# Three experts with at most 64 tokens in two passes, and one VectorE operation for the low part of each 1 MB load

## What is computed

```python
def swiglu(h, w1, w3, w2):
    return (jax.nn.silu(h @ w1) * (h @ w3)) @ w2

def moe_ffn(h, router, w1, w3, w2):
    t = h.reshape(B * S, D)                        # 256 x 1024
    logits = (t @ router).astype(jnp.float32)
    top_v, top_i = lax.top_k(logits, TOP_K)        # 2 of 8
    top_w = jax.nn.softmax(top_v, axis=-1)
    gates = jnp.sum(jax.nn.one_hot(top_i, N_EXPERTS) * top_w[..., None], axis=1)
    out = jnp.zeros_like(t)
    for e in range(N_EXPERTS):                     # D_FF_EXPERT = 3584
        out = out + gates[:, e:e + 1] * swiglu(t, w1[e], w3[e], w2[e])
    return out
```

## Time and profile before

| | us |
|---|---|
| median of 3 runs (1663.34 to 1664.61) | 1664.23 |
| the profiled execution's own time | 1664.06 |
| its span | 1662.0 |
| TensorE busy (matmuls) | 1616.8 |
| VectorE busy | 1300.9 |
| ScalarE busy | 1098.5 |
| GpSimd busy | 30.0 |

### The profile page before, as it was taken

The page is one execution under the profiler, slowest core; times in us unless marked ns, Lnnn a source line. Parts: engine busy times, 40 slices in busy tenths (PEclk is TensorE's granted clock), DMA queues, the critical chain, the costliest instruction groups (busy, mean ns, idle before and its releaser), DMA issues.

```text
span 1662.0 us, 23002 instructions
## 1 busy us (share of the span) xinstructions
PE 1616.8 (97%) x9056; PEld 1387.2 (83%) x9056; DVE 1300.9 (78%) x1411; ACT 1098.5 (66%) x1257; POOL 30.0 (2%) x37
## 2 busy tenths in 40 slices
PE   5999999999999996999999999999999999999998
PEld 5999869999899965888788788788788788788786
DVE  4887744555688654989889889889889889889886
ACT  4775343333567614878778778778778778778785
POOL 3000000000000003000000000000000000000000
PEclk9999999999999998999999999999999999999999
DMA  9555365555455547999999999999999999999990
GB/s 236 177 167 181 109 202 178 190 191 179 133 173 176 174 160 289 350 345 374 350 336 373 352 335 368 351 340 366 364 332 375 352 334 371 355 336 370 355 361 26
DMA packets 231398, 460.55 MB, mean 277 GB/s; under 512 B 7434, under 2 KB 79478, under 8 KB 231286
## 3 DMA queue, kind: packets, MB, share of 16 engines
q1 hardware_dynamic: 230262, 457.21, 78.1%
q0 software_dynamic: 832, 1.74, 0.7%
q10 hardware_dynamic: 192, 0.08, 0.0%
HBM read 457.96 MB, written 1.05 MB: 276 GB/s over the span
## 4 chain that ended last, share of the span: by engine, by line
PE 88%; DVE 4%; ACT 4%; DMA 3%; issue 1%; SPq 0%; ACTq 0%; DVEq 0%
PE bank L935 18%; PE bank L936 18%; PE bank L939 18%; PE bank L700 8%; PE bank L701 8%; PE bank L702 8%; PE bank L745 2%; PE bank L963 2%; DMA ring<-in_w_in 2%; PE bank L970 2%; PE bank L997 1%; ACT w_hi L507 1%; DVE w_lo L515 1%; DMA arena<-in_moe_w 1%; DVE shared8k L1685 1%; DVE prod L1683 1%
## 5 line engine op out<-in xcount | busy, mean ns | idle before, releaser
L551 DVE TENSOR_TENSOR w_lo<-arena,w_hi 128x1024 fp32r<-128x1024 f32 x486 | 579.4, 1220 | 82.3 <-ACT w_hi L545 70.8
L545 ACT ACTIVATE w_hi<-arena 128x1024 fp32r<-128x1024 f32 x492 | 517.7, 1061 | 168.7 <-PE bank L939 148.4
L935 PE MATMUL bank<-w_hi,h_hi 128*128 128x512 f32 x896 | 359.2, 401 | 3.2 <-DVE h_lo L1769 3.2
L936 PE MATMUL bank<-w_hi,h_lo 128*128 128x512 f32 x896 | 349.8, 390 | 0.0
L515 DVE TENSOR_TENSOR w_lo<-ring,w_hi 128x2048 fp32r<-128x2048 f32 x89 | 203.7, 2290 | 161.5 <-ACT w_hi L507 160.4
L700 PE MATMUL bank<-h_hi,w_hi 128*128 128x256 f32 x992 | 284.4, 287 | 8.0 <-DVE w_lo L515 6.3
L701 PE MATMUL bank<-h_lo,w_hi 128*128 128x256 f32 x992 | 281.6, 284 | 0.0
L702 PE MATMUL bank<-h_hi,w_lo 128*128 128x256 f32 x992 | 281.5, 284 | 0.0
L939 PE MATMUL bank<-w_lo,h_hi 128*128 128x512 f32 x896 | 276.9, 390 | 0.0
L507 ACT ACTIVATE w_hi<-ring 128x2048 fp32r<-128x2048 f32 x89 | 170.3, 1913 | 131.0 <-PE bank L702 80.8
L551 DVE TENSOR_TENSOR w_lo<-ring,w_hi 128x1024 fp32r<-128x1024 f32 x180 | 215.1, 1221 | 26.7 <-ACT w_hi L545 22.9
(11 more groups left out here) (239 smaller groups left out, 1659.8 us busy)
## 6 DMA issues: line engine op xcount, KB each, us to landing
arena<-in_moe_w SPq DMA_DIRECT2D x246, 1024.0 KB, 6.1
ring<-in_moe_w SPq DMA_DIRECT2D x90, 1024.0 KB, 6.4
ring<-in_ffn_w SPq DMA_DIRECT2D x33, 1024.0 KB, 5.2
ring<-in_w_gate SPq DMA_DIRECT2D x32, 1024.0 KB, 5.3
ring<-in_w_in SPq DMA_DIRECT2D x16, 1024.0 KB, 5.6
ring<-in_w_branch SPq DMA_DIRECT2D x8, 1024.0 KB, 4.8
ring<-in_w_out SPq DMA_DIRECT2D x8, 1024.0 KB, 4.8
x_tok<-in_x SPq DMA_DIRECT2D x2, 512.0 KB, 4.2
```

The lines of the kernel that those rows point to most:

```text
L545: nc.scalar.activation(half_hi[:, m % AHEAD, :], raw_of(n)[:, HALF * (m % 2):HALF * (m % 2) + HALF], ACT.Copy)\
L551: eng.tensor_tensor(half_lo[:, m % AHEAD, :], raw_of(m // 2)[:, HALF * (m % 2):HALF * (m % 2) + HALF], half_hi[:, m % AHEAD, :].bitcast(F3 ...
L935: pe.matmul(dst, hi, w[:, cols], start=first(x), stop=False)
L936: pe.matmul(dst, lo, w[:, cols], start=False, stop=False)
```

## The change

Expert 0 stays first. The other seven are put in an order that the counts set: the three with the fewest tokens go to positions 2, 4 and 6 (`SMALL`), the rest to 1, 3, 5 and 7. VectorE works out the order (the kernel's `order`, `perm` and `onehot`), permutes the columns of `chosen`, `place` and `gate` (`arrange`), and SyncE reads the expert's number from SBUF and puts it in the load's address (`expert`, `expert_drams`). `most_i` becomes the larger of the highest count and twice the third smallest of the seven, so that the same `If` with 128 also asks whether three of them have at most 64 tokens.

In positions 2, 4 and 6 the tokens take 64 columns. The gather writes them twice, the high part goes to columns 0 to 63 of `h_hi` and the low part to columns 64 to 127 of the same tile. One matmul with `w_hi` then gives hi by hi in rows 0 to 63 and lo by hi in rows 64 to 127; one with `w_lo` adds the rest. A half is four matmuls (`half_few`) where it was six. The two row groups have to be added. For h3 and w2 of such an expert that is done by later matmuls (`fold` in place of `ident`, and the spread with the gates written twice). For h1 it has to be done ahead of silu: ScalarE copies rows 64 to 127 to `prod`, VectorE adds rows 0 to 63, and ScalarE makes silu twice, for the upper and the lower rows.

VectorE's low part is made for a load at once (`split_load_lo`, 2048 columns), after both its halves have a high part; GpSimd's three first loads likewise. At the kernel's start unit 2 of `w_in` is issued ahead of the constants and parameters, and GpSimd's small loads wait for unit 1.

```diff
-        def split_half_lo(eng, m):
-            eng.wait_ge(half_hi_done, m + 1)
-            eng.tensor_tensor(half_lo[:, m % AHEAD, :], raw_of(m // 2)[:, HALF * (m % 2):HALF * (m % 2) + HALF],
-                              half_hi[:, m % AHEAD, :].bitcast(F32), ALU.subtract)\
-                .then_inc(half_lo_pool if ex.by_pool(m) else half_lo_dve, 1)
+        def split_load_lo(eng, n):
+            eng.wait_ge(half_hi_done, 2 * n + 2)
+            eng.tensor_tensor(w_lo[:, n % LO, :], raw_of(n), w_hi[:, n % HI, :].bitcast(F32), ALU.subtract)\
+                .then_inc(half_lo_pool if ex.by_pool(n) else half_lo_dve, 1)
...
-                if n == 2:
-                    sp.dma_start(par_rows[PC_CW:PC, :, :], conv_w.rearrange("l t (h p) -> (t h) l p", p=P)).then_inc(rows_loaded, 16)
...
                 sp.dma_start(ring[:, n % SLOTS, :].rearrange("p (k c) -> p k c", k=src.shape[1]), src)\
                     .then_inc(loaded[n % SLOTS], 16)
+                if n == 2:
+                    sp.dma_start(const[:, P:C_N], table[:, P:C_N]).then_inc(const_loaded, 16)
+                    sp.dma_start(par_rows[PC_CW:PC, :, :], conv_w.rearrange("l t (h p) -> (t h) l p", p=P)).then_inc(rows_loaded, 16)
...
+            def expert(e):
+                if e not in values:
+                    sp.wait_ge(perm_ready, 1)
+                    values[e] = sp.value_load(perm_i[0:1, e:e + 1], min_val=1, max_val=E - 1)
+                return values[e]
...
-                    for m in (2 * (n - RAW), 2 * (n - RAW) + 1):
-                        wait_half_lo(sp, m)
+                    wait_half_lo(sp, 2 * (n - RAW))
...
-            pool.wait_ge(loaded[0], 16)
+            pool.wait_ge(loaded[1], 16)
...
+            def half_few(m, outs, first, final):
+                pe.wait_ge(half_hi_done, m + 1)
+                w, wl = half_hi[:, m % AHEAD, :], half_lo[:, m % AHEAD, :]
+                for x, (both, cols, dst) in enumerate(outs):
+                    pe.matmul(dst, both, w[:, cols], start=first(x), stop=False)
+                wait_half_lo(pe, m)
+                for x, (both, cols, dst) in enumerate(outs):
+                    last = pe.matmul(dst, both, wl[:, cols], start=False, stop=final(x))
+                last.then_inc(half_used, 1)
...
# ScalarE
                     if done == ("h1", 1, 1):
                         act_e.wait_ge(half_used, u + 1)
+                        if i // S_MOE in SMALL:
+                            fn(prod[0:FEW, i % 2, :], bank[4 + i % 2][FEW:P, :], ACT.Copy).then_inc(z_copied, 1)
...
+                    if done == ("h3", 0, 1) and i // S_MOE in SMALL:
+                        act_e.wait_ge(z_added, few_steps(i) + 1)
...
+                        fn(sil[0:FEW, i % 2, :], prod[0:FEW, i % 2, :], ACT.Silu)
+                        fn(sil[FEW:P, i % 2, :], prod[0:FEW, i % 2, :], ACT.Silu).then_inc(sil_done, 1)
...
# VectorE
+            step(stt(out=cnt, in0=iota[:, 1:E], scalar=1.0 / 16, in1=counts[:, 1:E], op0=ALU.mult, op1=ALU.add))
...
+            ts(most_i[:, :], third[:, :], CAP / FEW, most[:, 0:1], ALU.mult, ALU.max).then_inc(most_ready, 1)
...
+                    if done == ("h3", 0, 0) and i // S_MOE in SMALL:
+                        dve.wait_ge(z_copied, few_steps(i) + 1)
+                        tt(prod[0:FEW, i % 2, :], bank[4 + i % 2][0:FEW, :], prod[0:FEW, i % 2, :], ALU.add).then_inc(z_added, 1)
                     if done == ("h3", 0, 0) and i >= 1:
                         lower(i - 1)
```

More of the change, by code:

```diff
@@ L46 @@
 AHEAD = 6
+SMALL = (2, 4, 6)
+FEW = 64
 MORE = 8
@@ L84, in shape_constants @@
     c[:, C_IOTA:C_IOTA + P] = np.arange(P)
+    by_count = list(SMALL) + [p for p in range(1, E) if p not in SMALL]
+    for r, p in enumerate(by_count):
+        c[:, C_WANT + p - 1] = r
     return c
@@ L359, in trunk_kernel @@
         most_i = sb("most_i", [P, 1], I32)
+        perm_i = sb("perm_i", [P, E], I32)
+        chosen_p = sb("chosen_p", [P, TT, E + 2])
+        place_p = sb("place_p", [P, TT, E + 2])
+        gate_p = sb("gate_p", [P, TT, E + 2])
+        third = sb("third", [P, 1])
+        OTHERS = E - 1
+        scratch = [prod[:, 1, 128 * i:128 * i + 128] for i in range(4)]
+        cnt = scratch[0][:, 0:OTHERS]
+        order = scratch[0][:, 16:16 + OTHERS]
+        last_small = scratch[0][:, 32:32 + OTHERS]
+        perm = scratch[0][:, 48:48 + OTHERS]
+        more = scratch[1][:, 0:OTHERS * OTHERS].rearrange("p (a b) -> p a b", a=OTHERS)
+        onehot = scratch[2][:, 0:OTHERS * OTHERS].rearrange("p (a b) -> p a b", a=OTHERS)
+        moved = scratch[3][:, 0:TT * OTHERS * OTHERS].rearrange("p (t a b) -> p t a b", t=TT, a=OTHERS)
         lgT = qk_raw[0:E, 0, :, :].rearrange("p i c -> p (i c)")[:, 0:T]
@@ L535, in wait_half_lo, with few_steps @@
         def wait_half_lo(eng, m):
-            eng.wait_ge(half_lo_pool if ex.by_pool(m) else half_lo_dve, ex.lo_count(m))
+            eng.wait_ge(half_lo_pool if ex.by_pool(m // 2) else half_lo_dve, ex.lo_count(m // 2))
+        def few_steps(i):
+            return sum(x // S_MOE in SMALL for x in range(i))
         def split_half_hi(m):
@@ L668, in _ @@
                                    pattern=[[0, 4], [-1, P]], channel_multiplier=1).then_inc(ws_lower, 1)
-            for m in range(ex.halves):
-                if ex.by_pool(m):
-                    split_half_lo(pool, m)
+            for n in range(len(ex.loads)):
+                if ex.by_pool(n):
+                    split_load_lo(pool, n)
         @block.tensor
```

173 lines of the change are left out of this document (133 added, 40 removed).

## The result

| | before | changed |
|---|---|---|
| median, us | 1663.78 (4 runs, 1663.06 to 1664.61) | 1647.88 (4 runs, 1645.52 to 1651.56) |
| profiled execution's span, us | 1662.0 | 1645.4 |
| mean granted clock of TensorE in that span | 0.992 | 0.984 |

The ratio is 0.9906, 95% interval 0.9887 to 0.9926: 15.9 us faster. The forecast was 1638.3 us, in a range of 1612 to 1658. The sign and the loop that holds the small steps came out as written, the gain is 16 us and not 26. The four runs of the changed kernel spread over 6 us. The four of before lie within 1.6, but 19 more of before, taken beside the first experiments, spread over 6 us too (1660.14 to 1666.29), so the spread is no mark of the change.

A forecast was written before the change was run, and what follows sets the result against it. TensorE bounds the kernel before; in small steps a VectorE and ScalarE loop of 16.65 us would. Small experts -24.8, start -2, normalization +1 make -25.8 against 1664.06: 1638.3 us, range 1612 to 1658.

The forecast's parts named there:

- The pace of the small steps: Small experts' steps: a VectorE and ScalarE loop of 16.65 us sets the pace, above TensorE's 12.4 and DMA's 16.3.
- the three signs of being wrong: ScalarE waits for loads in small experts, the clock is under 1.00 there, or normal experts take over 126 us.
- first matmul to the end of the first addition: Small expert's first step: from TensorE's first matmul to VectorE's first addition of the row groups, 8.9 us.
- six bare loops: Small expert: six loops of 16.65 us, each six low parts 13.2, product 0.60, addition 0.65, silu and high part 2.2.
- after the last addition, to the next expert: Small expert's end: 2.2 us, a low part of 2.2 and its matmuls of 1.35, 5.75 us in all.
- silu "0.50 us each by 923.03 - 922.53": Small steps: ScalarE makes silu twice after VectorE's addition, each taken as 0.50 us, within the 2.2 us before the low part.
- Rival 3: Small steps: TensorE's clock falls and the kernel is slower, 1685 us at two thirds of matmuls slow, 1753 at all; 7%.
- the point from which it decides: Share of a small step's matmuls at the lower clock where TensorE passes 16.65 us (0.44) or 17.85 us (0.56).
- the -2: Kernel's start: 2 us gained from the new load order, bounds 8.7 gained and 3 lost.
- The +1 for the normalization: Ahead of the experts: normalization waits for GpSimd's operations of twice the length, between 0 and 2.4 us, 1 lost taken.
- Rival 1: Small steps: tighter loop at VectorE's bare sum of 14.8 us, 1604 us, or likelier half of it, 1621; 16%.
- Rival 2: Looser loop, 0.9 us more wait per small step (1657 us), or the 0.8 us cover in normal steps fails (1649); 14%.

The follow-up runs named there:

- the filled kernel: Changed kernel plus TensorE matmuls whose results nobody reads, in every step of the small experts: 1643.68 us, ratio 0.9873; again 1643.78 us, 0.9882.
- The start alone: Kernel of before with only the new order of the loads at the start: 1660.47 us, ratio 0.9975.
- the merge alone: Kernel of before with only low parts of 2048 columns, on VectorE and GpSimd: 1664.06 us, ratio 1.000.

## Why the prediction was right, and where it was off

**The pace of the small steps: right.** They are VectorE's and ScalarE's loop, not TensorE's (12.4 us) and not DMA's. The wait stands where it was put, behind two silus and a high part: 2.09 us where some 1.8 were named. TensorE waits for VectorE there, and ScalarE for VectorE's addition and for no load. Of the three signs of being wrong that the prediction names, one came: the clock is 0.95 in the six loops and not 1.00. The other two did not (no wait for loads, 124.89 us for a normal expert). ScalarE's waits in the first small expert (892 to 1025; total, times, longest):

```profile
ACT qk_raw L1390 <- DVE prod L1940: 16.2, 7, 2.9
ACT w_hi L577 <- PE bank L975: 4.5, 10, 0.8
```

The addition is 0.60 from start to start (993.98 - 993.37), 0.65 was taken.

**A small expert: 122.17 us, not 118.0** (the first of the three, from its first matmul at 895.88 to the next expert's at 1018.05). Term by term:

| term | predicted | measured |
|---|---|---|
| first matmul to the end of the first addition | 8.9 | 9.2 |
| extra operations in six loops | 3.4 | 3.4 |
| six bare loops | 99.9 (16.65 each) | 101.5 (16.92 each) |
| TensorE's clock in the first loop | 0 | 0.9 |
| after the last addition, to the next expert | 5.75 | 6.33, and 0.8 with the clock low |
| sum | 118.0 | 122.1 |

(6.33 is from the filled kernel, where the same stretch runs at full clock: 1013.64 - 1007.31. The 0.8 is this expert's alone: behind the other two the clock did not fall.) The next expert should have spared 1.3 us, 1.8 for the matmuls less 0.5 for a late low part. From its first matmul to its gathering it takes 64.40 us in the filled kernel (1013.64 to 1078.04), a normal one 65.22 (770.99 to 836.21): 0.82 less. The late low part is there; what was left out is that eight transposes with `fold` take 0.81 us where four took 0.36.

The mis-sized term of the loop is **silu "0.50 us each by 923.03 - 922.53"**. That row is a silu on 128 rows. The new ones, on 64 rows and the same 512 columns, stand 0.65 us apart (994.08, 994.73, 995.38). Two of them make 0.30 us a loop more, which covers 16.92 - 16.65 = 0.27, and it is on the way out once more. The records themselves are nearly as long, 0.63 us against 0.60; the 128-row operation's successor starts 0.10 us before its end, the 64-row silu's 0.02 after. The old silu read PSUM and the new ones read SBUF, but a 64-row copy from PSUM has the same 0.62 from start to start (900.07, 900.69). Why was not tried.

**Rival 3 had its mechanism right and its place wrong.** The step that failed is the sentence that "the rows of this case show no swing at waits under 2 us". Between the first expert's first matmul at 657.79 and 1648 us the trace of before has no wait of TensorE at all, so its silence was no evidence. In the changed kernel the clock fell after waits of 1.77 to 2.05 us. The rule cited there, from the Trainium skill ("TensorE: Matmul & The Clock Gate", section "A second HAM failure mode: psum-queue depth-cycling"), that frequent short idle stretches make the clock swing, is borne out by the trace. But the price was 3.8 us and not 21 to 90: the falls were short, and in the middle steps they lay in TensorE's slack. The prediction had the point from which it decides (44% of a step's matmuls at the lower level); the middle steps stayed under it, and it did not ask about the first and the last step, where a fall costs at once (0.9 us in the first loop, 0.8 on the one way out where it came).

**The sum.** The experts gained 12.6 us in the trace where 24.8 was forecast. Of the 12.2 that are missing, silu's size took 18 x 0.27 = 4.9, the clock 3.8, the way in and out of three experts 3 x 0.88 = 2.6, and the next expert's first step 3 x 0.48 = 1.4. That is 0.5 too much, and the five normal experts give most of it back, 124.89 us each in place of 124.96. Ahead of the experts -1 was forecast (-2 and +1), and the two traces give -4.0, so an error the other way made up for some 3 us of this. The start alone measured -3.4 us, so the -2 was too small, inside its bounds of -8.7 and +3. The step that failed there is that unit 3 would find the same loads in the queues as before: it came 9.2 us earlier, in time, and unit 4 was the next to be late, which the prediction does not look at. The +1 for the normalization is about right. From its start to its second half, in the changed kernel:

```profile
627.69 0.16 DVE L1465 RECIPROCAL rstd<-rms 128x1 f32<-128x1 f32 x1 [0.46 <-ACT rms L1187]
627.89 5.43 DVE L1471 SCALAR_TENSOR_TENSOR shared8k<-x_tok,rstd,prod 128x512 f32<-128x512 f32 x2
633.25 0.15 DVE L1465 RECIPROCAL rstd<-rms 128x1 f32<-128x1 f32 x1
```

that is 5.56 us, against 4.84 in the trace of before (632.14 to 636.98): 0.7 more beside GpSimd's longer operations. Six of the seven other runs with the longer operations show 5.55 to 5.58, and one, the first with extra matmuls, 4.84.

**What the prediction had and did not see.** It credited the merge with 0.5 us less VectorE work in each step, and built the loop as it now runs, with the high part behind silu. It never asked what the loop would be with halves. That with halves the wait is 0.96 and not 2.09 us, so that the merge costs 21 us, only the experiment showed. Rival 1, a loop at VectorE's bare sum of 14.8 us, lost for this order of operations. With one high part moved ahead of the silus its bare loop runs at 15.13 to 15.16.

Rival 2's wait of 0.9 us in every small step and the failing cover in normal ones did not come: normal experts take 124.89 us, and the merge alone measured nothing. The order by counts and the `If` do what they say: the small experts run in positions 2, 4 and 6.

## What to carry to other kernels

When two engines feed each other in a loop, an operation that needs two of the other's results can start only when the second is there: merging two operations into one saves a fixed cost of 0.08 us here, and took away the half that would have covered a wait of 1.1 us. Before merging, look at what its producer has in its queue between the two halves, and put the short operation that someone waits for behind the piece that lets the partner go on; moving one operation ahead of two was worth 32 us, twice the whole change. Read a window of the loop for "busy of span" (94.0 of 105.8) first: while that gap stands, taking work off an engine helps only where the operation stands in the chain of waits. The silu that was left out stood in it (18 us); the 0.5 us a step that the merge took off VectorE did not, and the merge lost.

## What the runs showed of the hardware that was not expected

In the changed kernel the granted clock fell to its lower level after single waits of TensorE of 1.77 us (at 980.79), 1.78, 1.82 and 2.05, and not after each: in the same expert waits of 1.80 us (963.28) and 1.77 us (923.96) were followed by none.

```profile
963.28 0.72 PE L975 MATMUL bank<-w_lo,act_hi 128*128 128x512 f32 x2 [1.80 <-DVE w_lo L583]
```

What tells them apart is open. Once down, it stayed there some 3 to 4 us while TensorE worked without a pause (906 to 912 and 1016 to 1020). A ScalarE operation on 64 rows of 512 columns took 0.62 to 0.65 us from start to start, one on 128 rows 0.50, with nearly the same length of its record. And one VectorE operation of 2048 columns saves so little over two of 1024 (2.20 us against 2 x 1.14) that its length is a cost in itself as soon as anything waits for it.
